# A 31-tap depthwise convolution: twenty taps on sixteen 32-wide tiles of TensorE instead of fourteen on four 64-wide ones

## The chip, the cores and the metric

The kernel runs on one core of one Trainium2 chip. The metric is the device time of one execution in microseconds, from a run's start to its end; lower is better. A profiled execution gives a trace with the start and duration of each instruction.

## What is computed

The program is a whole network of transformer-like layers in float32 on 512 tokens of 1024 channels. The change touches one stage of it, the convolution of a "conformer" block:

```python
y = pointwise(h)                       # 1024 -> 2 x 1024: value and gate
y = value * sigmoid(gate)              # "glu", channels x tokens
y = conv_general_dilated(y, w_dw, padding=15 + 15, feature_group_count=1024) + b_dw   # 31 taps, each channel alone
y = silu(layernorm(y)) ; y = pointwise2(y)
```

Each channel has 31 weights of its own. Output token t of a channel is the sum over j of weight j times input token t + j - 15.

## The kernel before

Channels lie on the 128 partitions and the 512 tokens along a row, so the 1024 channels are eight groups of 128, numbered g = 0 to 7. The parity p = g % 2 chooses one of two buffers. The stage is called `p_1` and each engine walks through the eight groups in its own order; semaphores tie the engines together.

**TensorE** computes the pointwise product in `linear` (L2315): for a group 48 matmuls of 128x128 by 128x512, because each float32 product is split in three (`w_hi*H_hi`, `w_hi*H_lo`, `w_lo*H_hi`). The results, value and gate, go to a pair of banks of the PSUM tensor `G`. Behind the linear of group g it runs `taps(g-1)` (L1986, L1989): fourteen of the 31 taps as matmuls whose stationary operand is a diagonal matrix of weights, `tap_diag`. The array is split in four tiles of 64x64. A tile that reads the lower 64 partitions and writes the upper ones needs its input turned by 64 partitions, which is what `yp_turned` holds. The order on TensorE is therefore linear(0), linear(1), taps(0), linear(2), taps(1), ..., linear(7), taps(6), taps(7). Two banks of the PSUM tensor `M` per parity hold the sums of the taps; `taps(g)` waits until VectorE has added up group g - 2 (semaphore `cv_d`).

**ScalarE** rounds the weights that DMA brought to `w_hi` (L507, two chunks a group, each when TensorE has used the slot two groups back), computes the sigmoid of the gate (L2037) and makes `yp_turned` by two copies of 64 partitions (L2042).

**VectorE** subtracts to get `w_lo` (L512, two a group), multiplies value and sigmoid into the padded input `yp` (L2122), computes the seventeen taps that TensorE doesn't (L2129, L2131 and fifteen at L2135, in two sums `Y` and `S[:, 2]`), and adds the sums up: the previous group's low bank of `M` (L2111), its own two sums (L2139), the previous group's second bank (L2117).

**GpSimd** builds the diagonals for a group with two instructions (L2281, L2284).

After group 7, VectorE adds taps(7), and TensorE sums all eight groups of `Y` over the channels for the layer norm (L1998). The layer norm's other steps follow, then the second pointwise product `p_2`. TensorE's queue is in program order, so L1998 stands behind taps(7).

Of the kernel before, what the change touches and what calls it, by code (L numbers as in the profile page):

```python
# [12 lines left out]
ALU = mybir.AluOpType  # L13
# [116 lines left out]
def build(nc, a, out, consts):  # L130

    plan, chunks = linear_plan()
    with ExitStack() as ctx:
# [31 lines left out]
        def small(name, shape, dt=F32):  # L165
            n = 4
            for s in shape[1:]:
# [75 lines left out]
              for e, places in enumerate(((188 * K, 190 * K, 192 * K, 194 * K), (196 * K, 198 * K, 200 * K, 173 * K)))]  # L243
# [4 lines left out]
        tap_diag = at("tap_diag", 117 * K, [P, 2, PE_TAPS, HP])  # L248
        yp_turned = at("yp_turned", 125 * K, [P, 2, T + 2 * PAD])
        taps_turned = at("taps_turned", 130 * K, [P, 8 * HALF_TAPS])  # L250
        half_ident = at("half_ident", 131 * K, [P, HP])
# [65 lines left out]
                             "fin_c").split()]  # L317

# [1629 lines left out]

        def second_pe(pe, linear, linear_units, norm, from_h, squares_behind):
# [24 lines left out]
            def taps(g, p):  # L1974

                if g == 1:
                    pe.wait_ge(mod_ok, 4)
                pe.wait_ge(cv_w, 2 * g + 2)
                wait_read(pe, "p_1", g)
                pe.wait_ge(cv_x, 2 * g + 4)  # L1980
                pe.wait_ge(cv_d, g + 1)
                low, high = slice(0, HP), slice(HP, P)
                for j in range(HALF_TAPS):
                    here, there = V_TAPS + j, V_TAPS + HALF_TAPS + j
                    for hs, bank in ((low, 2 * p), (high, 2 * p + 1)):
                        pe.matmul(M[hs, bank, :], tap_diag[hs, p, j, :], yp[hs, p, here:here + T], start=(j == 0),  # L1986
                                  stop=(j == HALF_TAPS - 1), skip_group_check=True)
                    for hs, other, bank in ((low, high, 2 * p), (high, low, 2 * p + 1)):
                        mm = pe.matmul(M[other, bank, :], tap_diag[hs, p, HALF_TAPS + j, :],  # L1989
                                       yp_turned[hs, p, there:there + T], start=(j == 0), stop=(j == HALF_TAPS - 1),  # L1990
                                       skip_group_check=True)
                mm.then_inc(cv_pe, 1)
# [19 lines left out]
        def second_act(act):  # L2012
# [22 lines left out]
            def glu(i, p, g):  # L2035
# [52 lines left out]
        def second_dve(dve, link):  # L2088
# [10 lines left out]
            dve.memset(yp_turned[:], 0.0)  # L2099
            link(dve.memset(yp[:], 0.0))  # L2100
# [6 lines left out]
            def total_low(g, p):  # L2107

                dve.wait_ge(cv_pe, g + 3)
                y = Y[:, g, :]  # L2110
                dve.tensor_tensor(y, y, M[:, 2 * p, :], ALU.add).then_inc(cv_a, 1)  # L2111

            def total_high(g, p):

                dve.wait_ge(cv_a, g + 1)
                y = Y[:, g, :]
                dve.tensor_tensor(y, y, M[:, 2 * p + 1, :], ALU.add).then_inc(cv_d, 1)  # L2117

            def glu(i, p, g):
# [25 lines left out]
            total_low(DT - 1, 1)  # L2145
# [563 lines left out]
```

## Time and profile before

| what | value |
|---|---|
| time, median of 3 runs (lowest to highest) | 2609.1 us (2605.2 to 2610.09) |
| the profiled execution: its own time, its span | 2605.56 us, 2603.6 us |
| TensorE busy in the span | 97% |
| VectorE, ScalarE, GpSimd busy | 59%, 39%, 4% |
| granted TensorE clock, mean | 0.99 |
| stage `p_1` with its taps and sums | 2028.4 to 2175.3 us of the span |

Busy times overlap, since a matmul's record contains its passage through the array: two records one behind the other can cover each other. What a matmul takes of TensorE is read from the distance between starts, not from its duration. The same holds for the other engines, where records of neighbours overlap by about 0.1 us.

### The profile page before, as it was taken

How to read it: one execution, taken by the hardware profiler on the slowest of the kernel's cores; microseconds unless marked ns; L12 is line 12 of the kernel's file. 1: busy time of each engine (PE TensorE's matmuls, PEld its weight loads, DVE VectorE, ACT ScalarE, POOL GpSimd, SP SyncE). 2: the span in 40 equal slices, each digit the busy share in tenths (PEclk: the TensorE clock that was granted, in tenths of full speed). 3: DMA queues.
4: the chain of work that ended last, by engine and by line, in shares of the span. 5: the costliest groups of instructions: out<-in, count | busy, mean ns of one | idle time of the engine just before them, and what ended most of it. 6: DMA issues, size and time to landing. Idle time of an engine off the chain costs nothing.

```text
span 2603.6 us, 31523 instructions
## 1 busy us (share of the span) xinstructions
PE 2526.5 (97%) x12548; PEld 2009.1 (77%) x12548; DVE 1539.9 (59%) x2574; ACT 1027.5 (39%) x1581; POOL 98.0 (4%) x133
## 2 busy tenths in 40 slices
PE   7999999999999989999998998999999999999999
PEld 6887788888886667888876875888888665888887
DVE  6455675877455656646665255666653997534433
ACT  4344543434435555433345345323223324422323
POOL 0000001010000000000000000011100110000000
PEclk9998999999999999999999998999999999999999
DMA  5422335554221122332324220366652221233331
GB/s 156 131 82 80 91 98 170 155 175 138 66 86 52 58 73 73 97 97 89 95 91 127 82 69 22 122 195 193 193 154 89 65 65 41 88 96 95 97 97 54
DMA packets 285081, 266.86 MB, mean 102 GB/s; under 512 B 13332, under 2 KB 270664, under 8 KB 284936
## 3 DMA queue, kind: packets, MB, share of 16 engines
q1 hardware_dynamic: 268503, 210.33, 26.3%
q0 software_dynamic: 15024, 54.33, 7.0%
q8 instruction: 99, 1.62, 0.3%
q14 instruction: 47, 0.38, 0.0%
q10 hardware_dynamic: 1408, 0.20, 0.0%
HBM read 262.72 MB, written 2.10 MB: 102 GB/s over the span
## 4 chain that ended last, share of the span: by engine, by line
PE 86%; DVE 8%; ACT 3%; issue 2%; SPq 1%; DMA 0%; POOL 0%; ACTq 0%; DVEq 0%; POOLq 0%
PE G L2315 70%; PE G L2331 7%; DVE Y L2135 2%; PE M L2384 1%; DVE S L2135 1%; DVE w_lo L512 1%; PE M L808 1%; PE M L818 1%; PE M L1171 1%; PE M L1182 1%; PE M L2365 1%; PE M L1655 1%; PE M L1193 1%; PE M L1644 0%; ACT w_hi L507 0%
## 5 line engine op out<-in xcount | busy, mean ns | idle before, releaser
L512 DVE TENSOR_TENSOR w_lo<-raw,w_hi 128x1024 fp32r<-128x1024 f32 x396 | 484.3, 1228 | 660.6 <-ACT w_hi L507 659.8
L2315 PE MATMUL G<-H_hi,w_hi 128*128 128x512 f32 (+1 forms) x2016 | 803.1, 398 | 5.6 <-DVE H_lo L375 1.6
L2315 PE MATMUL G<-H_hi,w_lo 128*128 128x512 f32 (+1 forms) x2016 | 783.8, 389 | 0.0
L2315 PE MATMUL G<-H_lo,w_hi 128*128 128x512 f32 (+1 forms) x2016 | 783.8, 389 | 0.0
L507 ACT ACTIVATE w_hi<-raw 128x1024 fp32r<-128x1024 f32 x396 | 417.3, 1057 | 911.2 <-PE G L2315 806.4
L2315 PEld LDWEIGHTS G<-H_hi,w_hi 128*128 128x128 f32 x2016 | 380.5, 189 | 110.0 <-issue 29.4
L2315 PEld LDWEIGHTS G<-H_hi,w_lo 128*128 128x128 f32 x2016 | 379.9, 188 | 79.3
L2315 PEld LDWEIGHTS G<-H_lo,w_hi 128*128 128x128 f32 x2016 | 380.5, 189 | 78.5 <-issue 4.6
L2315 PE MATMUL G<-hid_hi,w_hi 128*128 128x512 f32 x864 | 337.8, 391 | 5.3 <-DVE hid_lo L631 3.9
L2315 PE MATMUL G<-hid_hi,w_lo 128*128 128x512 f32 x864 | 336.9, 390 | 0.0
L2315 PE MATMUL G<-hid_lo,w_hi 128*128 128x512 f32 x864 | 336.8, 390 | 0.0
L2315 PEld LDWEIGHTS G<-hid_hi,w_hi 128*128 128x128 f32 x864 | 162.6, 188 | 42.0 <-DVE hid_lo L631 5.6
L2315 PEld LDWEIGHTS G<-hid_hi,w_lo 128*128 128x128 f32 x864 | 162.5, 188 | 33.9
L2315 PEld LDWEIGHTS G<-hid_lo,w_hi 128*128 128x128 f32 x864 | 162.7, 188 | 33.6
L2331 PE MATMUL G<-w_hi,H_hi 128*128 128x256 f32 x480 | 139.8, 291 | 1.4 <-DVE H_lo L463 1.3
L610 DVE SCALAR_TENSOR_TENSOR S<-SQ,VT,S 128x511 f32<-128x511 f32 (+1 forms) x176 | 128.2, 749 | 19.4 <-ACT S L572 16.3
L2331 PE MATMUL G<-w_lo,H_hi 128*128 128x256 f32 x480 | 136.3, 284 | 0.0
L2331 PE MATMUL G<-w_hi,H_lo 128*128 128x256 f32 x480 | 136.3, 284 | 0.0
L692 DVE SCALAR_TENSOR_TENSOR mod_acc<-mod_w,cs,mod_acc 128x512 f32<-128x512 f32 x168 | 125.9, 750 | 3.4
L670 POOL DMA_DIRECT2D mod_w<-in_w_mod x96 | 69.7, 726 | 1055.2 <-DVE mod_acc L692 470.6
L2331 PEld LDWEIGHTS G<-w_hi,H_hi 128*128 128x128 f32 x480 | 92.4, 193 | 12.5 <-DVE H_lo L463 5.9
L572 ACT ACTIVATE S<-SQ,VT 128x512 f32<-128x512 f32 x88 | 67.1, 810 | 88.2 <-DVE SQ L617 88.2
(347 smaller groups left out, 2427.7 us busy)
## 6 DMA issues: line engine op xcount, KB each, us to landing
raw<-in_w_ff SPq DMA_DIRECT2D x128, 512.0 KB
mod_w<-in_w_mod POOLq DMA_DIRECT2D x96, 512.0 KB, 4.5
raw<-in_ffn_w_up SPq DMA_DIRECT2D x176, 256.0 KB
raw<-in_ffn_w_down SPq DMA_DIRECT2D x32, 512.0 KB
raw<-in_w_in SPq DMA_DIRECT2D x28, 512.0 KB
raw<-in_mlstm_w_in SPq DMA_DIRECT2D x24, 512.0 KB
raw<-in_kv_w SPq DMA_DIRECT2D x16, 512.0 KB
raw<-in_fox_w_qg SPq DMA_DIRECT2D x16, 512.0 KB
```

The lines of the kernel that those rows point to most:

```text
L507: act.activation(w_hi[:, j, :], raw[:, j, :], ACT.Copy).then_inc(hi_done, 1)
L512: dve.tensor_tensor(w_lo[:, j, :], raw[:, j, :], w_hi[:, j, :], ALU.subtract).then_inc(lo_done, 1)
L572: act.activation(S[:, h, :], SQ[:, h, :], ACT.Identity, bias=VT[:, ds(t + cb, 1)], scale=VT[:, ds(t + (cw + 88), 1)]).then_inc(f_a, 1)
L610: return dve.scalar_tensor_tensor(S[:, h, k:T], SQ[:, h, 0:T - k], w, S[:, h, k:T], ALU.mult, ALU.add)
L670: pool.dma_start(mod_w[:, n % 2], src[:, 2 * quarter:2 * quarter + 2, block * 512:block * 512 + 512]).then_inc(mod_landed[n % 2], 16)
L692: one = dve.scalar_tensor_tensor(acc[:, cols], w, c, acc[:, cols], ALU.mult, ALU.add)
L808: return pe.matmul(M[:, bank, col:col + T - s * P], mK[hs, h // 2, s * P:s * P + P], mQ[hs, h // 2, s * P:T], start=(col == 0), stop=True, ...
L818: mm = pe.matmul(M[:, 2 + b // 2, (b % 2) * (P + 1):(b % 2 + 1) * (P + 1)], m_part(h, s)[:, (b - s) * P:(b - s) * P + P], mV[:, s, h, :], ...
L1171: mm = pe.matmul(fox_scores(n, e)[:, 0:(b + 1) * P], xQ[hs, q, b * P:b * P + P], xK[hs, q, 0:(b + 1) * P], start=True, stop=True)
L2135: link.post(dve.scalar_tensor_tensor(acc, yp[:, p:p + 1, j:j + T], tap(j), acc, ALU.mult, ALU.add))
L2315: mm = pe.matmul(G[:, 2 * p + m, 0:n], lw[:, k, ms], rh[:, t, 0:n], start=(t == 0 and q == 0), stop=(t == st["ktiles"] - 1 and q == 2), sk ...
L2331: mm = pe.matmul(G[:, 2 * p + b // 2, (b % 2) * GC:(b % 2) * GC + GC], lh[:, t, bs], rw[:, k, :], start=(t == 0 and q == 0 and b % 2 == 0) ...
```

## The change

TensorE takes twenty taps and VectorE eleven. The array is split in sixteen tiles of 32x32. For that there are four copies of the input, turned by 0, 32, 64 and 96 partitions; copy d carries five of the taps, and its tile reads quarter r of the partitions and writes quarter r + d, into bank r of `M`. All four banks of `M` serve one group, so `taps(g)` now waits for the sums of group g - 1. The copies turned by 32 and 96 are made by four DMAs that ScalarE issues, the one turned by 64 by two ScalarE copies as before. The diagonals, 128x32 each, are built by twenty ScalarE instructions a group, and GpSimd's part goes. VectorE adds four banks instead of two. Before the first group ScalarE makes a 32-wide identity and the turned weights in sixteen small instructions, where it had two.

```diff
-PE_TAPS = 14
-HALF_TAPS = PE_TAPS // 2
+COPIES, COPY_TAPS = 4, 5
+PE_TAPS = COPIES * COPY_TAPS
 V_TAPS = CONV_K - PE_TAPS
+QP = P // COPIES
...
-                pe.wait_ge(cv_w, 2 * g + 2)
+                pe.wait_ge(cv_w, g + 1)
                 wait_read(pe, "p_1", g)
-                pe.wait_ge(cv_x, 2 * g + 4)
-                pe.wait_ge(cv_d, g + 1)
...
-                for j in range(HALF_TAPS):
-                    here, there = V_TAPS + j, V_TAPS + HALF_TAPS + j
-                    for hs, bank in ((low, 2 * p), (high, 2 * p + 1)):
-                        pe.matmul(M[hs, bank, :], tap_diag[hs, p, j, :], yp[hs, p, here:here + T], start=(j == 0),
...
+                pe.wait_ge(cv_x, 2 * g + 2)
+                pe.wait_ge(cv_r[p], 64 * (g // 2 + 1))
+                pe.wait_ge(cv_d, g + 2)
+                for j in range(COPY_TAPS):
+                    for d in range(COPIES):
+                        source = yp_turned[d - 1] if d else yp
+                        tap = V_TAPS + COPY_TAPS * d + j
+                        for r in range(COPIES):
+                            rs, cs = quarter(r), quarter(r + d)
+                            mm = pe.matmul(M[cs, r, :], tap_diag[rs, p, COPY_TAPS * d + j, :], source[rs, p, tap:tap + T],
+                                           start=(j == 0), stop=(j == COPY_TAPS - 1), skip_group_check=True)
                 mm.then_inc(cv_pe, 1)
...
+                for d, parts in ((1, ((0, 96, 32), (96, P, 0))), (3, ((32, P, 0), (0, 32, 96)))):
+                    for first, end, source in parts:
+                        act.dma_start(yp_turned[d - 1][first:end, p, PAD:PAD + T],
+                                      yp[source:source + end - first, p, PAD:PAD + T]).then_inc(cv_r[p], 16)
                 for to, hs in ((slice(HP, P), slice(0, HP)), (slice(0, HP), slice(HP, P))):
-                    act.activation(yp_turned[to, p, PAD:PAD + T], yp[hs, p, PAD:PAD + T], ACT.Copy).then_inc(cv_x, 1)
...
+                    act.activation(yp_turned[1][to, p, PAD:PAD + T], yp[hs, p, PAD:PAD + T], ACT.Copy).then_inc(cv_x, 1)
+                for d in range(COPIES):
+                    for j in range(COPY_TAPS):
+                        col = ROW["w_dw_2"] + 8 * (V_TAPS + j) + g
+                        w = taps_turned[:, d - 1, 8 * j + g:8 * j + g + 1] if d else VT[:, col:col + 1]
+                        one = act.activation(tap_diag[:, p, COPY_TAPS * d + j, :], quarter_ident[:], ACT.Copy, scale=w)
+                one.then_inc(cv_w, 1)
+
+            for r in range(COPIES):
+                act.activation(quarter_ident[quarter(r), :], ident[quarter(r), quarter(r)], ACT.Copy).then_inc(cv_h, 1)
+                for d in range(1, COPIES):
+                    first = ROW["w_dw_2"] + 8 * (V_TAPS + COPY_TAPS * d)
+                    act.activation(taps_turned[quarter(r), d - 1, :], VT[quarter(r + d), first:first + 8 * COPY_TAPS],
+                                   ACT.Copy).then_inc(cv_h, 1)
+            act.wait_ge(cv_h, 16)
             groups(act, "p_1", split_hi, glu)
...
+            for tile in yp_turned + [yp]:
+                dve.memset(tile[:, :, 0:PAD], 0.0)
+                one = dve.memset(tile[:, :, PAD + T:], 0.0)
...
+            def total(g, r):
+
+                if r:
+                    dve.wait_ge(cv_a, 3 * g + r)
+                else:
+                    dve.wait_ge(cv_pe, g + 3)
                 y = Y[:, g, :]
...
                 if g:
-                    total_low(g - 1, 1 - p)
+                    total(g - 1, 0)
                 dve.tensor_tensor(y, y, other, ALU.add).then_inc(cv_v, 1)
                 if g:
-                    total_high(g - 1, 1 - p)
+                    for r in range(1, COPIES):
+                        total(g - 1, r)
...
             groups(dve, "p_1", split_lo, glu)
-            total_low(DT - 1, 1)
-            total_high(DT - 1, 1)
+            for r in range(COPIES):
+                total(DT - 1, r)
```

TensorE, where the linear of group 1 ends and taps(0) begins. A row's name is the source line, the instruction, what it writes and reads, the size of what it writes, and how many like it follow one another. Before:

```order
L2315 MATMUL G<-H_hi,w_hi 128x512
L2315 MATMUL G<-H_lo,w_hi 128x512
L2315 MATMUL G<-H_hi,w_lo 128x512
L1986 MATMUL M<-yp,tap_diag 64x512 x2
L1989 MATMUL M<-yp_turned,tap_diag 64x512 x2
```

and with the change, where the three turned copies bear the numbers 148 to 150:

```order
L2320 MATMUL G<-H_hi,w_hi 128x512
L2320 MATMUL G<-H_lo,w_hi 128x512
L2320 MATMUL G<-H_hi,w_lo 128x512
L1995 MATMUL M<-yp,tap_diag 32x512 x4
L1995 MATMUL M<-yp_turned_148,tap_diag 32x512 x4
L1995 MATMUL M<-yp_turned_149,tap_diag 32x512 x4
L1995 MATMUL M<-yp_turned_150,tap_diag 32x512 x4
```

The pair of tap rows stood seven times, 28 matmuls on four tiles; the four new tap rows stand five times, 80 matmuls on sixteen tiles. The linears are untouched.

ScalarE, from the last weight chunk before the stage on. Before:

```order
L507 ACTIVATE w_hi<-raw 128x1024
L2046 ACTIVATE taps_turned<-VT 64x56 x2
L507 ACTIVATE w_hi<-raw 128x1024 x2
L2037 ACT_TABLE_LOAD
L2037 ACTIVATE S<-G,VT 128x512
L2042 ACTIVATE yp_turned<-yp 64x512 x2
L507 ACTIVATE w_hi<-raw 128x1024 x2
```

and with the change, from the last of the four quarters of the small instructions on:

```order
L2060 ACTIVATE quarter_ident<-ident 32x32
L2063 ACTIVATE taps_turned<-VT 32x40 x3
L510 ACTIVATE w_hi<-raw 128x1024 x2
L2042 ACT_TABLE_LOAD
L2042 ACTIVATE S<-G,VT 128x512
L2048 DMA yp_turned_148<-yp 96x512
L2048 DMA yp_turned_148<-yp 32x512
L2048 DMA yp_turned_150<-yp 96x512
L2048 DMA yp_turned_150<-yp 32x512
L2051 ACTIVATE yp_turned_149<-yp 64x512 x2
L2056 ACTIVATE tap_diag<-quarter_ident,VT 128x32 x5
L2056 ACTIVATE tap_diag<-quarter_ident,taps_turned 128x32 x15
```

Sixteen small instructions now stand ahead of the stage's first weight chunk, and four DMA issues and twenty diagonals between a group's sigmoid and the next group's weight chunks.

VectorE, at the end of a group. Before:

```order
L2135 SCALAR_TENSOR_TENSOR S<-yp,VT,S 128x512
L2135 SCALAR_TENSOR_TENSOR Y<-yp,VT,Y 128x512
L2111 TENSOR_TENSOR Y<-Y,M 128x512
L2139 TENSOR_TENSOR Y<-Y,S 128x512
L2117 TENSOR_TENSOR Y<-Y,M 128x512
L512 TENSOR_TENSOR w_lo<-raw,w_hi 128x1024 x2
```

and with the change:

```order
L2156 SCALAR_TENSOR_TENSOR S<-yp,VT,S 128x512
L2156 SCALAR_TENSOR_TENSOR Y<-yp,VT,Y 128x512
L2134 TENSOR_TENSOR Y<-Y,M 128x512
L2160 TENSOR_TENSOR Y<-Y,S 128x512
L2134 TENSOR_TENSOR Y<-Y,M 128x512 x3
L515 TENSOR_TENSOR w_lo<-raw,w_hi 128x1024 x2
```

Two more additions of banks stand there, and of the rows of the first kind nine a group instead of fifteen.

## Rows read from the trace of the kernel before

**Rows 1.** The page, busy time of each engine: us, share of span, instructions.

```profile
PE 2526.5 (97%) x12548; PEld 2009.1 (77%) x12548; DVE 1539.9 (59%) x2574; ACT 1027.5 (39%) x1581; POOL 98.0 (4%) x133
```

**Rows 2.** taps(0) to taps(6): length, PE, PEld, DVE, ACT, POOL busy; PEclk, DMA, GB/s.

```profile
2050.37:2154.01 103.64, 103.64 (x625) 65.76 (x624) 103.18 (x142) 23.77 (x30) 13.86 (x12) 1.00 0.21 62
```

**Rows 3.** The timeline of TensorE around taps(4): start, duration, instruction, count.

```profile
2119.47 0.65 PE L1986 MATMUL M<-yp,tap_diag 64*64 64x512 f32 x2
...
2125.10 0.59 PE L1986 MATMUL M<-yp,tap_diag 64*64 64x512 f32 x2
2125.11 0.59 PE L1989 MATMUL M<-yp_turned,tap_diag 64*64 64x512 f32 x2
```

**Rows 4.** The timeline of VectorE over group 4.

```profile
2107.66 0.75 DVE L2122 SCALAR_TENSOR_TENSOR yp<-G,VT,S 128x512 f32<-128x512 f32 x1
2108.44 0.55 DVE L2129 TENSOR_SCALAR Y<-yp,VT 128x512 f32<-128x512 f32 x1
2108.90 1.18 DVE L2131 TENSOR_SCALAR S<-yp,VT 128x512 f32<-128x512 f32 x1
...
2119.32 0.73 DVE L2135 SCALAR_TENSOR_TENSOR S<-yp,VT,S 128x512 f32<-128x512 f32 x1
2119.99 0.73 DVE L2135 SCALAR_TENSOR_TENSOR Y<-yp,VT,Y 128x512 f32<-128x512 f32 x1
2120.75 0.69 DVE L2111 TENSOR_TENSOR Y<-Y,M 128x512 f32<-128x512 f32 x1
2121.36 0.68 DVE L2139 TENSOR_TENSOR Y<-Y,S 128x512 f32<-128x512 f32 x1
...
2122.56 2.36 DVE L512 TENSOR_TENSOR w_lo<-raw,w_hi 128x1024 fp32r<-128x1024 f32 x2
```

**Rows 5.** TensorE with four 32-wide column tiles, elsewhere in the program.

```profile
1970.71 2.78 PE L731 MATMUL M<-mod_acc,ones 128*32 128x512 f32 x24
```

**Rows 6.** TensorE with small matmuls in a row, elsewhere in the program.

```profile
1410.61 3.08 PE L1524 MATMUL G<-rm,sel 128*64 128x64 f32 x98
```

**Rows 7.** The timeline of ScalarE: small instructions at three places, then the stage's start.

```profile
104.15 0.40 ACT L954 ACTIVATE mL<-mN,gates_T 128x128 f32<-128x128 f32 x1
104.45 0.56 ACT L956 ACTIVATE mL<-M,gates_T 128x384 f32<-128x384 f32 x1
...
689.52 1.57 ACT L2539 ACTIVATE xV<-G,root_T 128x256 f32<-128x256 f32 x4 [5.98 <-DVE root_T L2619]
...
2037.29 0.53 ACT L2046 ACTIVATE taps_turned<-VT 64x56 f32<-64x56 f32 x2
...
2039.66 1.06 ACT L507 ACTIVATE w_hi<-raw 128x1024 fp32r<-128x1024 f32 x1 [0.75 <-PE G L2315]
...
2042.04 0.69 ACT L2037 ACTIVATE S<-G,VT 128x512 f32<-128x512 f32 x1
2043.99 1.29 ACT L2042 ACTIVATE yp_turned<-yp 64x512 f32<-64x512 f32 x2 [1.27 <-DVE yp L2122]
```

**Rows 8.** DMAs that ScalarE issues: timeline of two issues; size and landing.

```profile
1.61 0.34 ACTq L2186 DMA_DIRECT2D v_rows<-in_norm_mix_pre  x1
1.98 0.44 ACTq L2186 DMA_DIRECT2D v_rows<-in_norm_mix_post  x1
...
ident<-const_ident ACTq DMA_DIRECT2D x1, 64.0 KB, 3.9
```

**Rows 9.** The timeline of TensorE at the stage's end.

```profile
2161.49 0.65 PE L1986 MATMUL M<-yp,tap_diag 64*64 64x512 f32 x2 [1.23 <-ACT yp_turned L2042]
...
2167.66 6.28 PE L1998 MATMUL G<-Y,ones 128*128 128x512 f32 x14
2174.12 1.13 PE L1998 MATMUL G<-Y,ones 128*128 128x512 f32 x2 [0.19 <-DVE Y L2117]
```

**Rows 10.** Stretches around an idle TensorE, columns as in rows 2.

```profile
1370.70:1374.20 3.50, 0.01 (x1) 0.00 (x0) 2.36 (x2) 1.02 (x4) 2.95 (x6) 1.00 0.56 132
1375.30:1378.60 3.30, 3.30 (x11) 2.27 (x10) 0.08 (x1) 1.32 (x2) 0.00 (x0) 0.50 0.86 344
```

More of the change, by code:

```diff
@@ L247, in build @@
         yp = at("yp", 112 * K, [P, 2, T + 2 * PAD])
[L248 to L251, printed above, removed]
+        yp_turned = [at(f"yp_turned{d}", 117 * K + 4608 * (d - 1), [P, 2, T + 2 * PAD]) for d in range(1, COPIES)]
+        tap_diag = at("tap_diag", 131 * K, [P, 2, PE_TAPS, QP])
+        taps_turned = at("taps_turned", 136 * K + 128, [P, COPIES - 1, 8 * COPY_TAPS])
+        quarter_ident = at("quarter_ident", 137 * K, [P, QP])
         G = ctx.enter_context(nc.psum_tensor("G", [P, 4, 512], F32))
@@ L317, in build @@
                              "fin_c").split()]
+        cv_r = [sem(f"cv_r{p}") for p in range(2)]
         TOKENS = [(hid_l, 1), (cv_pe, 2), (cv_d, 2)]
@@ L2098, in second_dve @@
             dve.wait_ge(chunk_used, used_after("s0_down3"))
-            dve.memset(yp_turned[:], 0.0)
-            link(dve.memset(yp[:], 0.0))
+            for tile in yp_turned + [yp]:
+                dve.memset(tile[:, :, 0:PAD], 0.0)
+                one = dve.memset(tile[:, :, PAD + T:], 0.0)
+            link(one)
             dve.wait_ge(mod_ok, 3)
@@ L2105, in second_dve @@
             mod_rest(dve, link, 1)
-            def total_low(g, p):
-                dve.wait_ge(cv_pe, g + 3)
-                y = Y[:, g, :]
[L2111 to L2117, printed above, removed]
+            def total(g, r):
[3 more added lines that the diff above has]
+                    dve.wait_ge(cv_pe, g + 3)
+                y = Y[:, g, :]
+                one = dve.tensor_tensor(y, y, M[:, r, :], ALU.add)
+                if r == COPIES - 1:
+                    one.then_inc(cv_d, 1)
+                else:
+                    one.then_inc(cv_a, 1)
             def glu(i, p, g):
@@ L2269, in _ @@
             pool_mod(pool)
-            pool.wait_ge(chunk_used, used_after("s0_down3"))
-            taps = VT[:, ROW["w_dw_2"]:ROW["w_dw_2"] + 8 * CONV_K].rearrange("p (j t) -> p j t", t=8)
-            turned = taps_turned[:].rearrange("p (j t) -> p j t", t=8)
-            pool.tensor_tensor(half_ident[:], ident[:, 0:HP], ident[:, HP:P], ALU.add).then_inc(cv_h, 1)
-            pool.wait_ge(cv_h, 1)
-            pool.wait_ge(cv_x, 2)
-            each = half_ident[:].unsqueeze(1).to_broadcast([P, HALF_TAPS, HP])
-            for t in range(DT):
-                p = t % 2
-                pool.wait_ge(cv_pe, t + 1)
-                pool.tensor_tensor(tap_diag[:, p, 0:HALF_TAPS], each,
-                                   taps[:, V_TAPS:V_TAPS + HALF_TAPS, t:t + 1].to_broadcast([P, HALF_TAPS, HP]),
-                                   ALU.mult).then_inc(cv_w, 1)
-                pool.tensor_tensor(tap_diag[:, p, HALF_TAPS:PE_TAPS], each,
-                                   turned[:, :, t:t + 1].to_broadcast([P, HALF_TAPS, HP]),
-                                   ALU.mult).then_inc(cv_w, 1)
         @block.tensor
```

12 lines of the change are left out of this document (2 added, 10 removed).

## The prediction

> **What bounds the kernel now.** I read the busy times first [rows 1]: TensorE is busy 97% of the span and no other engine over 59%, so over the whole program TensorE's own work sets the time. The stage has a balance of its own. Between the starts of taps(0) and taps(6), six groups, TensorE is busy 103.64 of 103.64 us and VectorE 103.18, at full clock [rows 2]. Both are full, so neither may lose work alone and save much. A group takes 103.64 / 6 = 17.27 us.
>
> In the timeline of TensorE [rows 3] taps(4) starts at 2119.47 and its last burst at 2125.10. Fourteen bursts, four records on the four tiles within some 0.02 us, are thirteen distances of (2125.10 - 2119.47) / 13 = 0.433, so I take 0.43 a burst. A float32 matmul goes through in two passes, hence seven tap rounds are fourteen bursts: 14 x 0.43 = 6.02. The rest of the group, linear and the two changes of tiling, is 17.27 - 6.02 = 11.25 us.
>
> In VectorE's timeline [rows 4] a tap costs 0.66 from start to start (2119.32 to 2119.99) and an addition 0.61. L2131 takes 1.18 where a like one needs some 0.45, since GpSimd builds diagonals at that moment. The whole group is, in distances of starts: 0.78 for yp, 0.46, 0.39, 0.7 of that disturbance, 15 x 0.663 = 9.95, 0.1 until the last tap is written, 3 x 0.6 = 1.8 and 2.3 for the two w_lo: 16.5. So VectorE is 0.8 us shorter than TensorE, and TensorE decides the group.
>
> **TensorE's part of the change.** 80 matmuls in two passes on sixteen tiles are ten bursts instead of fourteen, if all sixteen tiles run at once. The nearest row is L731 [rows 5]: four column tiles of 32, each with an input of its own, 24 records in 2.78 us. With 0.6 for the last one, five distances of (2.78 - 0.6) / 5 = 0.436: four different inputs stream at the same time from the same partitions at no loss. Rows of different quarters at once are what the 64-wide tiles do already [rows 3]. Both ways together are in no row; I take 0.43 a burst, 4.30, and 0.08 more for starting sixteen tiles one behind the other. Upper bound by issue: L1524 [rows 6] issues 98 records in 3.08 us, (3.08 - 0.22) / 97 = 29.5 ns a record together with its weight load; 160 of them would be 4.72. The page of the Trainium skill "TensorE: Matmul & The Clock Gate", Part 3, measured sixteen 32x32 tiles at 10.6 times the speed of one, one burst and not float32; it speaks for full overlap, and by it the sum stays as it is.
>
> The group becomes 11.25 + 4.38 = 15.63, which saves 1.64. Over six distances: 9.8 us.
>
> **Does another engine stand in the way of 15.63?** VectorE loses six taps (6 x 0.663 = 3.98) and GpSimd's 0.7 and gains two additions. The last two wait for the write of the one before, so 0.72 each instead of 0.6: 16.5 - 3.98 - 0.7 + 1.44 = 13.3. ScalarE has, a group: sigmoid 0.67, two w_hi 2.1, copies 1.3 [rows 7], four DMA issues at 0.37, the distance in [rows 8], 1.5, and twenty diagonals. A 128x32 instruction with a weight per partition is in no row. L954, 128x128 with such an operand, stands 0.30 before its neighbour, and L2539 does 256 columns in (1.57 - 0.46) / 3 = 0.37 [rows 7]. The difference is 0.0006 a column, so 32 columns are 0.24 us, or less where the fixed part is smaller; I take 0.2, 4.0 for twenty; bounds 0.1 and 0.3. Together 9.6 of 15.6. The new wait for group g - 1 is a ring too: taps(g), linear(g+2), w_hi 1.1, w_lo 1.2, VectorE's group 11.0, and only then taps(g+2): 4.4 + 11.2 + 2.3 + 11.0 = 28.9 for two groups, 14.5 each. Nothing there reaches 15.63. The DMAs land 3.9 us after issue [rows 8], while taps(g) comes over 10 us after yp(g): hidden.
>
> **The start.** The sixteen small instructions stand ahead of the first w_hi. Two of 64x56 took 0.53 [rows 7], so I take 0.24 each, 3.8 instead of 0.5. Behind them ScalarE had 0.75 of idle time before the second w_hi, and sigmoid ended at 2042.73 for a yp that started at 2043.22. So yp(0) comes 3.3 - 0.75 - 0.5 = 2.05 late, at 2045.3, and ends at 2046.05. Then DMA issues 1.5, copies 1.3, diagonals 4.0: 2052.8, when linear(1) has ended at 2050.3. taps(0) starts 2.4 late. The landing of the DMAs (2047.6 + 3.9 = 2051.5) is just below. Memsets are shorter by some 1.5 us, but VectorE waits there for the norm's row.
>
> taps(6) then starts at 2052.8 + 6 x 15.63 = 2146.6 instead of 2154.01: 7.4 earlier.
>
> **The end**, where I expect the gain to be given back. Before, taps(7) ran at 2161.49 under VectorE's last group, and fourteen of the sixteen records of L1998 under it as well; from taps(6) to the last sum went 2175.25 - 2154.01 = 21.2 us [rows 9]. With the change taps(7) must wait until VectorE has emptied `M` of group 6, which it does at the end of its group 7. From the start of taps(6), when linear(7) has just ended: w_hi and w_lo 2.4, VectorE's group 0.78 + 0.46 + 0.39 + 5.97 + 0.1 + 0.6 + 0.6 + 0.6 + 1.44 = 10.9, so 13.3 until taps(7), then 4.4 bare, and then L1998 with all sixteen records, 15 x 0.43 + 0.6 = 7.05, since it is queued behind taps(7). VectorE's four last additions, 2.7, lie beside L1998. Sum 24.75.
>
> TensorE is idle for 13.3 - 4.4 = 8.9 us before taps(7). After 3.5 us without work at 1370.7 the granted clock of the next stretch is 0.50, the lower of the two levels, and it stays there for 3.4 us [rows 10]. So taps(7) begins at half clock, for 3.4 to 6.8 us, of which half is lost: 1.7 to 3.4, I take 2.5. The same page of the skill, Part 1, says that an idle TensorE falls to 1.2 GHz and comes back when busy; the trace agrees. The end takes 27.2, 6.0 more than before.
>
> **Sum.** -7.4 + 6.0 = -1.4 us. Against the profiled execution's own 2605.56 that is 2604.2. The median of the runs, 2609.1, lies 3.5 above that execution, and the runs span 4.9, so I put the forecast at 2609.1 - 1.4, about 2607.5. A measurement of this kernel can tell 0.2%, 5.2 us, from nothing.
>
> Bounds of the likeliest case. Issue at 29.5 ns instead of 26.9: 0.42 x 7 = +2.9. Diagonals at 0.3: +2; at 0.1: -1.3, since the DMAs land then. Small instructions at 0.1: -2 (not both, PE is ready at 2050.3; together -2.4). DMA issues at 0.5 (the longer record of [rows 8] is 0.44): +0.5. Clock: -0.8 or +0.9. From -1.4 this gives -4.6 to +4.9, all within 0.2%. Chance 0.54.
>
> **Rivals.** (a) Sixteen tiles do not overlap fully. L731 shows four column tiles, L1986 two by two; should only eight run at once, there are twenty bursts, 8.6 us, and with 4.3 more in seven places the kernel takes +30, 2638. From a burst of 0.48 on (seven times 0.5 = 3.5 more, with the upper ends above) it is slower. Full halving 0.10; a partial loss, 0.5 to 0.55 a burst, +5 to +8, 0.13. (b) The instructions aren't brought up in time. The skill's same page, Part 1, gives some 62 ns a matmul where microcode decodes. As a mechanism here: 160 records at 62 ns are 9.9 us, 5.5 more in seven places, +39, 2647; the 29.5 ns of [rows 6] speak against it, 0.03. (c) Faster: the start is hidden (taps(0) at 2050.4, -2.4) and the low clock falls to its short end or away (-0.8 to -2.5): -4.6 to -6.3, and a little less per burst passes the mark; 2602. For it speaks that full-width small instructions overlap by 0.1 us; against it that two partial ones did not. 0.19. (d) ScalarE becomes late with w_hi: with issues of 0.5 and diagonals of 0.3 its group is 0.67 + 2.1 + 1.3 + 2.0 + 6.0 = 12.1, still under 15.6. w_hi would be 1 to 2 us late in a group that has over 2 to spare: 0.01 beyond the mark. (e) A cost nobody sees in these rows, such as more waits on TensorE or DMA traffic against `raw`: in the range.
>
> So faster 0.19, same 0.54, slower 0.27. The likeliest case spans 2603 to 2614.5; with the partial loss of (a) and with (c) the range that leaves out two in ten is 2601 to 2617.
>
> **What would show it.** In the profile after: starts of taps(1) to taps(6) 15.6 us apart; sixteen records within about 0.1 us and bursts 0.43 apart; a taps(7) that waits for VectorE's L2134 and lies bare before L1998 at clock 0.50; diagonals 0.2 apart; the first taps near 2052.8. I am wrong if a burst takes over 0.48, if TensorE waits for VectorE or ScalarE within the six groups, or if the clock stays at full level in the end.

## The result and the profile after

The changed kernel takes 2614.55 us (median of 8 runs, 2612.26 to 2616.71), the kernel before 2605.48 (8 runs, 2604.84 to 2610.09). The ratio is 1.003, with a 95% interval of 1.0019 to 1.0041: slower by 0.3%, some 9 us. The forecast was 2607.5 and no measurable change. It was counted from 2609.1, the median of three runs; from the 2605.48 of eight the same sum, -1.4, gives 2604.1, so the miss is some 10 us. The execution that was profiled is the longest of the eight, span 2614.9 against 2603.6; where its other microseconds lie is said below.

The page of the changed kernel first, its busy times (us, share of the span, instructions), to be held against [rows 1]:

```profile
PE 2525.2 (97%) x13380; PEld 2016.7 (77%) x13380; DVE 1509.8 (58%) x2548; ACT 1064.0 (41%) x1755; POOL 77.7 (3%) x116
```

TensorE has 832 records more and 1.3 us less of busy time, VectorE 30 us less. Nothing of that can be read as time, so I went to the stage. TensorE's timeline of the changed kernel, the group of taps(4) from its first burst to the next linear (start, duration, instruction, count, and in brackets the idle time before it and what ended it):

```profile
2125.05 0.63 PE L1995 MATMUL M<-yp,tap_diag 32*32 32x512 f32 x4
2125.08 0.69 PE L1995 MATMUL M<-yp_turned,tap_diag 32*32 32x512 f32 x12
2125.50 0.61 PE L1995 MATMUL M<-yp,tap_diag 32*32 32x512 f32 x4
2125.53 0.66 PE L1995 MATMUL M<-yp_turned,tap_diag 32*32 32x512 f32 x12
2125.93 0.83 PE L1995 MATMUL M<-yp,tap_diag 32*32 32x512 f32 x4
2126.18 0.79 PE L1995 MATMUL M<-yp_turned,tap_diag 32*32 32x512 f32 x12
...
2127.01 0.82 PE L1995 MATMUL M<-yp,tap_diag 32*32 32x512 f32 x4
2127.23 0.80 PE L1995 MATMUL M<-yp_turned,tap_diag 32*32 32x512 f32 x12
...
2130.50 0.50 PE L2320 MATMUL G<-H_hi,w_hi 128*128 128x512 f32 x1
```

The first two bursts are as the prediction has them: sixteen records (4 + 12) within 0.1 us, the next sixteen 0.45 later. So sixteen tiles do stream at once. From the third burst on they don't begin together any more: of the four records of `yp` the first begins at 2125.93, on time, the other three from 2126.13 on (the row lasts 0.83 instead of 0.61), and the twelve of `yp_turned` from 2126.18. From there a round of sixteen tiles, two bursts, takes 1.05 to 1.06 (2126.18 to 2127.23) and not 0.86, so 0.20 more. The taps take 2130.50 - 2125.05 = 5.45 us, where the prediction has 4.38. Before it was 6.17 up to the next linear (2119.47 in [rows 3] to 2125.64): fourteen bursts of 0.43, 6.02, and some 0.15 for the change to the linear. Counted like that the new taps are ten bursts, 4.30, the same 0.15, and 1.0 that is new.

The weight loads show what is late. A load that stands alone, on time, and the next one:

```profile
2125.94 0.10 PEld L1995 LDWEIGHTS M<-yp,tap_diag 32*32 32x32 f32 x1 [0.33 <-issue]
2126.12 0.10 PEld L1995 LDWEIGHTS M<-yp,tap_diag 32*32 32x32 f32 x1
```

Each late matmul begins 4 ns after the start of its load. Their turn, 0.43 behind the burst before, was at 2125.93 to 2126.03, so they wait for their weights.

The same kernel's start and end in TensorE's timeline: the first linear, the first records of taps(0) and taps(7), and the sums; taps(1) begins at 2075.39 and taps(6) at 2158.16.

```profile
2031.26 0.47 PE L2320 MATMUL G<-H_hi,w_hi 128*128 128x512 f32 x1 [0.64 <-DVE H_lo L378]
...
2057.28 1.08 PE L1995 MATMUL M<-yp,tap_diag 32*32 32x512 f32 x4 [4.00 <-ACT tap_diag L2056]
...
2171.75 1.08 PE L1995 MATMUL M<-yp,tap_diag 32*32 32x512 f32 x4 [8.08 <-DVE Y L2134]
...
2179.43 7.13 PE L2003 MATMUL G<-Y,ones 128*128 128x512 f32 x16
```

Two waits are new, 4.00 us ahead of taps(0) for ScalarE's diagonals and 8.08 ahead of taps(7) for VectorE's totals. The records behind either last 1.08 instead of 0.63: the clock is low. The windows view says it too (length, then busy time of TensorE, its weight loads, VectorE, ScalarE, GpSimd, granted clock, DMA share, GB/s):

```profile
2057.30:2060.60 3.30, 3.30 (x64) 1.20 (x65) 2.32 (x3) 2.40 (x3) 0.00 (x0) 0.50 0.02 6
2075.39:2158.16 82.77, 82.77 (x1042) 58.82 (x1041) 65.96 (x95) 41.08 (x125) 0.00 (x0) 1.00 0.32 94
...
2171.75:2176.60 4.85, 4.85 (x89) 2.15 (x97) 0.00 (x0) 0.00 (x0) 0.00 (x0) 0.50 0.01 3
```

The second row is five groups at full clock: TensorE busy throughout, VectorE 65.96 of 82.77. Before, both were full [rows 2]. VectorE is off the bound, and 82.77 / 5 = 16.55 is TensorE's own group.

**Where the time went**, in stretches of the profiled executions, with linear(0) at 2028.42 before and 2031.26 after:

| stretch | before | after | difference |
|---|---|---|---|
| linear(0) to taps(0) | 21.95 | 26.02 | +4.07 |
| taps(0) to taps(1) | 17.27 | 18.11 | +0.84 |
| taps(1) to taps(6), five groups | 86.37 | 82.77 | -3.60 |
| taps(6) to the end of the sums | 21.24 | 28.41 | +7.17 |
| together | 146.83 | 155.31 | +8.5 |

The 8.5 agree with the 9 us between the medians. The span has 2.8 more ahead of linear(0), and that isn't the change's: in the profiles of the variants below linear(0) starts anywhere from 2027.01 to 2031.54, with the same TensorE program ahead of it. The granted clock of earlier stages differs from one execution to the next. Of 165 us from 1305 on, its mean is 0.99 in the profile before and 0.97 in the one after. The same hole in the same program shows how: an idle time of 2.21 us near 1404, first before, then after.

```profile
1403.16 3.40 PE L2384 MATMUL M<-SQ,ones 128*128 128x512 f32 x7 [2.21 <-ACT SQ L442]
```

```profile
1405.55 1.22 PE L2389 MATMUL M<-SQ,ones 128*128 128x512 f32 x1 [2.21 <-ACT SQ L445]
```

Behind it the granted clock is 1.00 before and 0.50 after (windows 1405.3 to 1408.7). Of the fourteen profiles of this case six have it full there and eight low, though what they differ in comes 600 us later. So I compare stretches counted from linear(0) between profiles, and totals only over many runs.

### The profile page after: what moved, and what is told of

The parts are those of the page before. It is cut to its first block, busy times and chain, and to the rows that moved or that the text cites. A ratio compares the mean times of both kernels' runs of the same rounds, so it can differ in the third digit from the quotient of the medians.

```text
span 2614.9 us, 33348 instructions
## 1 busy us (share of the span) xinstructions
PE 2525.2 (97%) x13380; PEld 2016.7 (77%) x13380; DVE 1509.8 (58%) x2548; ACT 1064.0 (41%) x1755; POOL 77.7 (3%) x116
## 4 chain that ended last, share of the span: by engine, by line
PE 90%; DVE 4%; ACT 3%; issue 2%; SPq 1%; DMA 0%; ACTq 0%; POOL 0%; DVEq 0%; POOLq 0%
PE G L2320 73%; PE G L2336 7%; PE M L1995 2%; PE M L2389 1%; PE M L811 1%; PE M L821 1%; PE M L1185 1%; PE M L1174 1%; PE M L1196 1%; PE M L2370 1%; PE M L1658 1%; ACT w_hi L510 1%; PE M L1647 0%; DVE S L613 0%; PE M L2395 0%
```

## Experiments on the taps

Three questions stood after the result: why a group's taps take 5.45 and not 4.38, what the start costs, what the end costs. "Issue" means here that TensorE can't take in its instructions faster; "overlap" that sixteen tiles stream more slowly than four.

**Half the columns.** This kernel leaves out TensorE's twenty taps for the second half of the tokens.

```diff
-  mm = pe.matmul(M[cs, r, :], ..., source[rs, p, tap:tap + T],
+  mm = pe.matmul(M[cs, r, 0:GC], ..., source[rs, p, tap:tap + GC],
```

> The tap matmuls stream 256 columns instead of 512, so half of every token row gets no TensorE taps (part of the computation is left out); everything else is as with the change. It asks what sets the 5.45 us that 80 tap matmuls take where 4.3 were forecast. Theory (issue): behind the first two bursts TensorE gets a record with its weight load only every 33.4 ns, whatever it streams, so 160 records still take 4.4 to 5.4 us from the first tap to the next linear. Rival (overlap): sixteen tiles streaming at once slow each other, on the input side or in PSUM; half the columns are then half the time, about 2.7 us.

The first record and the next linear, in its TensorE timeline:

```profile
2068.89 0.42 PE L1995 MATMUL M<-yp,tap_diag 32*32 32x256 f32 x4
...
2072.20 0.50 PE L2320 MATMUL G<-H_hi,w_hi 128*128 128x512 f32 x1
```

3.31 us, neither of the two. Both theories fell as I had stated them. The two points fit a cost per column and a fixed part: (5.45 - 3.31) / 256 columns = 8.36 ns for the 160 records together, 4.28 at 512, which is ten bursts of 0.43; and 1.17 beside it. Of that 0.15 is the change to the linear that the kernel before has too; the other 1.0 is 0.20 for each of the five rounds. (The group of taps(5) took 3.95 there at full clock, which I can't explain; the other full-clock ones are alike.)

**A quarter of the columns**, `0:P` in the same place, tests that line with a third point; it leaves out three quarters of the tokens.

> As the half-column run, with 128 of 512 columns streamed (three quarters of every row get no TensorE taps, part of the computation left out). 512 columns took 5.45 us from the first tap to the next linear and 256 took 3.32, so neither pure issue nor pure overlap loss holds. Theory (additive): the tiles stream as forecast, 8.3 ns a column over ten bursts, and 1.19 us are fixed, 0.24 for each of the five rounds of sixteen tiles, because the next round's weight loads come up late: 2.26 us. Rival (supply): a record with its weight load needs at least some 20.7 ns, which 256 columns just reached: 3.3 us again.

```profile
2070.93 0.31 PE L1995 MATMUL M<-yp,tap_diag 32*32 32x128 f32 x4
...
2073.19 0.50 PE L2320 MATMUL G<-H_hi,w_hi 128*128 128x512 f32 x1
```

2.26. The line gives 1.17 + 128 x 0.00836 = 2.24. And 160 records with their loads go in 2.26 us, 14 ns each, half of the 29.5 that I had worked out of [rows 6] as a bound of issue: that row never was one for small tiles. The late rows of `yp_turned` agree without the line: from the second round on they follow each other 0.63 apart with 256 columns and 0.42 with 128, where two bursts of the stream are 0.43 and 0.21. The surplus is 0.20 a round at all three widths. (Two of the six full-clock groups took 4.1; in one of them TensorE has a hole of 1.54 us ahead of the last thirteen records, put down to issue. I left it there.)

It doesn't follow the clock either. In the kernel with early totals, below, taps(0) ran at half clock (0.50 from 2054.9 to 2060.7), and two rounds follow each other like this:

```profile
2056.84 1.24 PE L1995 MATMUL M<-yp_turned,tap_diag 32*32 32x512 f32 x12
...
2058.77 1.24 PE L1995 MATMUL M<-yp_turned,tap_diag 32*32 32x512 f32 x12
```

That is 1.93, where two bursts take 1.70 at this clock: a surplus of 0.23, not of 0.40.

**Eight tiles at a time.** The computation is complete; the loop goes twice over the five taps, for d = 0, 1 and for d = 2, 3.

```diff
-  for j in range(COPY_TAPS):
-      for d in range(COPIES):
+  for half in range(2):
+      for j in range(COPY_TAPS):
+          for d in (2 * half, 2 * half + 1):
```

> The same 80 tap matmuls in another order: two halves, each five rounds over eight tiles, so that only eight tiles can run at once; the computation is complete. It asks what the fixed 0.24 us a round hang on. Theory (a round of sixteen tiles holds 64 instructions, weight loads and matmuls of two passes, and TensorE sees only a limited number of them ahead, so the next round's loads begin late): with eight tiles the next round is always within reach, twenty bursts of 0.43 and almost nothing on top, 8.6 to 8.8 us from the first tap to the next linear. Rival (every burst pays for starting its tiles one behind the other, 0.12 for sixteen): half of that for eight, twenty times 0.49, 9.8 us. Either way the kernel becomes slower, by 7 times 3.2 us or more.

```profile
2094.49 0.63 PE L1996 MATMUL M<-yp,tap_diag 32*32 32x512 f32 x4
...
2096.66 0.61 PE L1996 MATMUL M<-yp,tap_diag 32*32 32x512 f32 x4
...
2102.64 0.50 PE L2322 MATMUL G<-H_hi,w_hi 128*128 128x512 f32 x1
```

Five bursts in 2096.66 - 2094.49 = 2.17, 0.434 each, and all records of a burst begin on time. 8.15 for the twenty bursts is less than 20 x 0.434, since the second half's tiles begin under the end of the first. With eight tiles the first half shows no surplus at all.

**Twelve tiles.** This one leaves out the five taps of the last copy.

```diff
-  for d in range(COPIES):
+  for d in range(COPIES - 1):
```

> Leaves out the five taps of the third turned copy (d = 3): a round has twelve tiles, five rounds, 120 records a group. Question: to what does the 0.24 us belong that a round of sixteen tiles takes beyond its two bursts (1.09 against 0.86), and that a round of eight does not take. Theory A, the reach of the queue: the loads of the next round come late because a round of sixteen puts 64 instructions (32 loads, 32 matmuls) between a tile's matmul and its next load; a round of twelve has 48, and the surplus is gone or small: 5 x 0.87 = 4.35 us from the first record to the next linear, at most 4.6. Rival B, a cost per tile above eight: half the surplus, 0.12 a round, about 4.95 us. Rival C, a cost of every round in which all four row quarters and all four column quarters carry three or more tiles: the whole surplus, 5.45 us. The time itself says little, since taps(7) and the end keep their chain.

```profile
2091.12 0.63 PE L1995 MATMUL M<-yp,tap_diag 32*32 32x512 f32 x4
2091.15 0.66 PE L1995 MATMUL M<-yp_turned,tap_diag 32*32 32x512 f32 x8
...
2092.01 0.60 PE L1995 MATMUL M<-yp,tap_diag 32*32 32x512 f32 x4
2092.03 0.88 PE L1995 MATMUL M<-yp_turned,tap_diag 32*32 32x512 f32 x8
...
2092.86 0.61 PE L1995 MATMUL M<-yp,tap_diag 32*32 32x512 f32 x4
...
2095.98 0.50 PE L2320 MATMUL G<-H_hi,w_hi 128*128 128x512 f32 x1
```

4.86, by the number rival B's (4.95), by the rows neither's. The rounds begin 0.85 to 0.89 apart (2091.12, 2092.01, 2092.86), so no round loses anything; but from the second round on part of the tiles begin late (the row of eight records lasts 0.88 instead of 0.66), and that lag is paid once, at the end: 4.86 - 5 x 0.86 - 0.15 = 0.41. With sixteen the lag is paid in every round. So twelve tiles keep the 0.43 of a burst and sixteen don't. Per record sixteen are still faster, 34.1 ns over a group to 40.5, where 0.43 a burst would be 27. The reach of the queue had forecast at most 4.6 here: it fits the rhythm of the rounds and misses the lag at the end.

**Another order of the sixteen**: along rows of the array instead of diagonals, the rest as it was, computation complete.

```diff
-  for d in range(COPIES):
-      ...
-      for r in range(COPIES):
+  for r in range(COPIES):
+      for d in range(COPIES):
```

> Complete computation; within a round of sixteen tiles the order alone is changed: four tiles of one row quarter follow one another (columns r, r+1, r+2, r+3), where the changed kernel walks along diagonals. The number of instructions between a tile's matmul and its next load stays 64. Theory A (reach of the queue): nothing changes, 5.45 us a group from the first record to the next linear (5.35 to 5.55). Rival C (the surplus comes from tiles that follow one another on different rows and columns, or from output banks written by turns): the surplus goes or doubles, 4.4 or over 5.8 us. Time as the changed kernel by A, 2614 within 4.

5.45 from the first record to the next linear (2075.34 to 2080.79), as by the reach of the queue; rival C's other order does nothing. One run, 2616.81 us.

**Where the loads stop.** In the second round the loads pause behind the first tiles, and they begin again 0.03 us after the first record of the second burst has ended, counted from a group's first record: at 1.07 for 1.04 with 512 columns, at 0.65 for 0.62 with 256, at 0.43 for 0.40 with 128, at 1.94 for 1.91 at half clock, and with twelve tiles again at 1.07 for 1.04, each time with 33 or 34 loads begun. With eight tiles the first half has no such pause. So in these rows the loads wait for a matmul of the round before to be finished, which is what a limited reach of the queue would do. No run changes that reach alone, so it stays the likeliest reading and not a shown one.

## Experiments on the start and the end

**The totals of group g - 1 between VectorE's own taps**, so that `M` comes free earlier:

```diff
   link.post(dve.scalar_tensor_tensor(acc, yp[...], tap(j), acc, ...))
+  if g and 4 <= j < 8:
+      total(g - 1, j - 4)
 ...
-  if g:
-      total(g - 1, 0)
 ...
-  if g:
-      for r in range(1, COPIES):
-          total(g - 1, r)
```

> VectorE adds the four banks of the previous group between its own taps 4 to 8, each behind one tap, instead of at the end of the group; the same work. Theory (the end is a serial chain: VectorE's last group, bare taps(7), sums): taps(7) starts about 10.5 us after taps(6) instead of 13.6, the end shrinks by about 3 us, and the six groups before don't change, since TensorE sets them (16.55 each). Against the changed kernel -3 to -4 us, that is a ratio to the kernel before of about 1.002. Rival (the end is set by TensorE's sixteen sums and the low clock): taps(7) comes earlier but the low clock covers the same stretch, less than 1 us.

2613.71 us (7 runs, 2612.43 to 2615.34), ratio to before 1.0027 [1.0017, 1.0037]: hardly a gain over the changed kernel's 1.003, where 3 to 4 us were expected. From taps(6) to the sums' end 26.66 instead of 28.41, so 1.75 less, and taps(7) begins 12.0 behind taps(6) and not 10.5. Its timeline of ScalarE, last group, and the first row of taps(7) in TensorE's:

```profile
2160.06 3.06 ACTq L2048 DMA_DIRECT2D yp_turned<-yp  x4
...
2164.48 1.17 ACT L2056 ACTIVATE tap_diag<-quarter_ident,VT 128x32 f32<-128x32 f32 x5
2165.55 3.27 ACT L2056 ACTIVATE tap_diag<-quarter_ident,taps_turned 128x32 f32<-128x32 f32 x15
```

```profile
2168.88 1.08 PE L1995 MATMUL M<-yp,tap_diag 32*32 32x512 f32 x4 [6.48 <-ACT tap_diag L2056]
```

VectorE is done with `M` at 2167.37, but now taps(7) waits for ScalarE until 2168.82. Behind the wait that I cured stood another, which ends 1.45 us later: 3.06 us of DMA issues, 1.3 of copies and 4.3 of diagonals.

**The sums of blocks 0 to 5 ahead of taps(7)**, in the idle time:

```diff
+  if g == DT - 1:
+      wait_read(pe, "p_1", DT - 2)
+      group_sums(0, DT - 2)
 ...
-  for t in range(DT): ...
+  group_sums(DT - 2, DT).then_inc(cv_s, 1)
```

> TensorE computes the layer norm's sums over groups 0 to 5 in the idle time ahead of taps(7), and only those of groups 6 and 7 behind it; the same work. Theory (queue order and clock): 12 of 16 records of 0.43 us leave the bare end, and TensorE rests under 3.5 us, so that the granted clock stays at its upper level: from taps(6) to the last sum 28.4 us become about 22.9, VectorE's four additions being last. Against the changed kernel -5 to -6 us, ratio to before about 1.001. Rival: VectorE's additions set the end already and the clock stays low: -1 us.

2611.10 us (12 runs, 2607.13 to 2614.46), 1.0016 [1.0007, 1.0025]. The end takes 25.62. Its TensorE timeline:

```profile
2162.53 5.42 PE L1983 MATMUL G<-Y,ones 128*128 128x512 f32 x12
2170.67 1.08 PE L2004 MATMUL M<-yp,tap_diag 32*32 32x512 f32 x4 [2.72 <-DVE Y L2139]
...
2177.54 1.13 PE L1983 MATMUL G<-Y,ones 128*128 128x512 f32 x2
2180.63 2.08 PE L1983 MATMUL G<-Y,ones 128*128 128x512 f32 x2 [1.96 <-DVE Y L2139]
```

Six of eight sums are off the end, 5.4 us, but 2.8 net remain of it, and 5 to 6 were expected. The expectation that under 3.5 us of rest the clock would stay up was wrong: taps(7) begins at half clock after 2.72 us of idle time, and takes 6.87 for 5.45. The last sum now waits 1.96 for the last total, and it runs at half clock too, 2.08 for two records where the two ahead of it took 1.13.

**ScalarE's sixteen small instructions between the fills of `H_hi`**, two behind each, instead of ahead of the first group's w_hi:

```diff
+  for t in range(DT):
+      fill_act(act, "odd", ..., (t,))
+      ...  # two of quarter_ident and taps_turned
-  for r in range(COPIES):
-      act.activation(quarter_ident...)
-      ...
```

> The sixteen small ScalarE instructions stand two by two in the gaps of the fill before the stage instead of in one row ahead of the first weight chunk; the same work. [...] Against the changed kernel -3 to -5 us. Rival: the fill has no room (gaps of 0.6 us for two instructions of 0.25), the linear starts later by what the taps win: 0.

**The four DMAs of a group from GpSimd's queue** instead of ScalarE's:

```diff
 (act)  -  act.dma_start(yp_turned[d - 1]..., yp...)
 (pool) +  for g in range(DT):
        +      wait_read(pool, "p_1", g); pool.wait_ge(cv_pe, g + 1)
        +      ...  pool.dma_start(yp_turned[d - 1]..., yp...)
```

> GpSimd, idle here, issues the four DMAs of a group instead of ScalarE; the same work. They took 2.5 to 3.3 us of ScalarE's time where the forecast had 1.5. Theory: at the start the chain yp(0), issues, copies, diagonals loses its 2.5 us, so taps(0) starts 2 to 2.5 us earlier (a little less if GpSimd's own issue and landing then decide), the six groups stay at 16.62 us from taps to taps, the end stays too, since VectorE decides it: -2 to -3 us against the changed kernel, ratio to before about 1.002. Rival: landing is late from GpSimd's queue and takes the place of the issues: 0.

2610.27 us (11 runs, 2607.00 to 2613.15), 1.0016 [1.0008, 1.0025], and 2609.52 (11 runs, 2606.88 to 2611.28), 1.0013 [1.0004, 1.0022]. The first row of taps(0) in the timeline of the one and of the other:

```profile
2051.99 0.63 PE L1995 MATMUL M<-yp,tap_diag 32*32 32x512 f32 x4 [1.46 <-ACT tap_diag L2067]
```

```profile
2052.03 0.63 PE L1995 MATMUL M<-yp,tap_diag 32*32 32x512 f32 x4 [1.43 <-ACT tap_diag L2052]
```

Each alone brings taps(0) from 26.02 to 23.50 and 23.46 behind linear(0). The second gain is the clock: after an idle time of 1.4 us it stays at full level (0.63 for the row of four records), after 4.00 it had fallen, and taps(0) to taps(1) is 16.56 and 16.58 instead of 18.11. The two gains together are 4.1 us in either kernel.

**Sixteen taps on TensorE**, four of each copy, `COPY_TAPS = 4`, fifteen on VectorE; complete.

> Four taps a copy instead of five: TensorE takes sixteen taps, VectorE fifteen; nothing else. Theory (round of sixteen tiles 1.09 us, stream 0.86 plus 0.23): taps take 4 x 1.09 = 4.4 us on TensorE, whose group would be 15.5; VectorE's is 13.3 + 4 x 0.66 = 15.9 and decides: 15.9 to 16.1 from taps to taps instead of 16.55. ScalarE builds sixteen diagonals: the start is 0.9 earlier. The end: VectorE's last group 2.6 longer, taps(7) 1.1 shorter. Against the changed kernel -3.3 - 0.9 + 1.5 = -2 to -4 us. Rival (the ring through the new wait for group g - 1 decides: taps, linear, w_hi, w_lo, VectorE's group of 13.6): over 16.5 a group and 0 or slower in all.

2611.95 us (11 runs, 2608.05 to 2614.71), 1.0019 [1.0010, 1.0028]. The taps take 4.38, and 5.45 - 4.38 = 1.07 is one round less, as the surplus says. But taps(1) already waits for VectorE, and taps(2) too:

```profile
2072.48 0.63 PE L1995 MATMUL M<-yp,tap_diag 32*32 32x512 f32 x4 [1.92 <-DVE Y L2134]
...
2088.37 0.63 PE L1995 MATMUL M<-yp,tap_diag 32*32 32x512 f32 x4 [0.31 <-DVE Y L2134]
```

The group is 79.47 / 5 = 15.89, VectorE's and not 15.5, and the end grows to 30.08, since VectorE's last group has four taps more. taps(0) has 3.07 us of idle time ahead of it; its first 0.8 us run at full clock and the next 3.4 at half, so the clock fell behind the hole and not in it.

**All four cures at once**, with twenty taps and with sixteen; the edits are those above.

> Twenty taps on sixteen tiles as changed, with the four cures together: totals early, sums of groups 0 to 5 first, small instructions in the fill's gaps, DMAs from GpSimd. Theory (start and end gave the gain back, the six groups keep 0.7 us each): start as before the change, six groups -4.3, end 20 to 21.5 instead of 21.2: -4 to -5 us against the kernel before, ratio 0.998 to 0.9985. Rival (the cures overlap in what they cure, and the low clock takes the rest): within 0.1% of before.

> The four cures and sixteen taps instead of twenty on TensorE. Theory: start as before the change, six groups of 15.95 instead of 17.27, -7.9 us, end about 19.6 to 21 instead of 21.2: -8 to -9.5 us against the kernel before, ratio 0.9965 to 0.997. Rival (VectorE, now full, is slowed by its neighbours or by the ring): groups of 16.5, ratio 0.9985.

Twenty taps: 2602.26 us (11 runs, 2599.99 to 2604.05), ratio to before 0.9987 [0.9978, 0.9996]. Sixteen: 2602.07 (11 runs, 2598.57 to 2606.68), 0.9986 [0.9977, 0.9995]. Both are faster than the kernel before by 3 us, a small gain that the interval just sets apart from none, and by the ratios some 11 us faster than the changed kernel. With twenty taps 4 to 5 us below the kernel before were expected; the stretches of the profile give 4.8, the medians 3.3. With sixteen, 8 to 9.5 were expected, and that missed. The end with twenty, then with sixteen:

```profile
2148.44 0.63 PE L2004 MATMUL M<-yp,tap_diag 32*32 32x512 f32 x4
...
2153.89 5.42 PE L1983 MATMUL G<-Y,ones 128*128 128x512 f32 x12
2159.24 0.63 PE L2004 MATMUL M<-yp,tap_diag 32*32 32x512 f32 x4
...
2164.69 1.12 PE L1983 MATMUL G<-Y,ones 128*128 128x512 f32 x2
2167.77 1.37 PE L1983 MATMUL G<-Y,ones 128*128 128x512 f32 x2 [1.96 <-DVE Y L2140]
```

```profile
2161.23 1.08 PE L2004 MATMUL M<-yp,tap_diag 32*32 32x512 f32 x4 [5.66 <-DVE Y L2140]
```

With twenty, taps(6), the early sums and taps(7) join without a hole and at full clock; the end takes 20.70. With sixteen the group is shorter (77.70 / 5 = 15.54), but VectorE, whose own group is 15.76, is late at the end: taps(7) waits 5.66 and begins at half clock, 26.11. So the two come out alike.

The stretches of all complete kernels, us; the total runs from linear(0) to the end of the sums:

| kernel | to taps(0) | to taps(1) | to taps(6) | to the sums' end | total |
|---|---|---|---|---|---|
| before | 21.95 | 17.27 | 86.37 | 21.24 | 146.83 |
| changed | 26.02 | 18.11 | 82.77 | 28.41 | 155.31 |
| totals early | 26.05 | 19.26 | 82.77 | 26.66 | 154.74 |
| sums first | 26.04 | 19.30 | 82.77 | 25.62 | 153.73 |
| small ones earlier | 23.50 | 16.56 | 82.77 | 28.77 | 151.60 |
| DMAs from GpSimd | 23.46 | 16.58 | 82.77 | 28.47 | 151.27 |
| eight tiles | 26.03 | 20.88 | 96.31 | 31.63 | 174.85 |
| sixteen taps | 25.11 | 19.00 | 79.47 | 30.08 | 153.66 |
| four cures, 20 | 21.97 | 16.55 | 82.77 | 20.70 | 141.99 |
| four cures, 16 | 21.98 | 15.50 | 77.70 | 26.11 | 141.29 |

In the two rows with 19.26 and 19.30 the clock was low at taps(0) for 6.8 us and not for the 3.4 of the changed kernel's profile, behind the same wait of 4.0; the edits there don't touch it. It makes their totals 1.2 us too long.

## Why the prediction was wrong

The sum said -1.4; counted the same way it is +8.5. It forecast no measurable change, and the kernel became slower by 9 us. The 9.9 between the sums, step by step:

- **"I take 0.43 a burst, 4.30, and 0.08 more": the step that failed.** Sixteen tiles stream at once, as said, but each round costs 0.20 beside its two bursts, and the 0.08 was meant for the whole group: 5.45 for 4.38, of which 0.15 is the change to the linear that my 11.25 already held. A group is 16.55 where 15.63 was forecast, 0.92 in each of six distances, +5.5, and once more in the end, +1.07. My upper bound, 4.72 from the rate of [rows 6], didn't cover it, because that rate has nothing to do with this case: the quarter-column kernel goes at 14 ns a record. It is rival (a) in its partial form, 0.545 a burst, to which I gave 13 in 100 and +5 to +8.
- **The rule on sixteen tiles.** The rows above show one burst of sixteen complete, its records starting over 0.10 us, and the third one broken. The Trainium skill, "TensorE: Matmul & The Clock Gate", Part 3, measured one burst, and for one burst the trace agrees with full overlap. Rounds one behind the other are not in it, and I carried it over to them. What its 10.6 of sixteen means for a row of rounds I didn't ask.
- **The start, 2.4 late: the right chain, too short.** It is 4.07. The four DMA issues took 2.53 where I had four distances of 0.37, +1.0; the diagonals 4.35 for 4.0, the small instructions 4.1 for 3.8. Together +1.65. ScalarE's timeline of the changed kernel:

```profile
2040.25 0.75 ACT L2063 ACTIVATE taps_turned<-VT 32x40 f32<-32x40 f32 x3
...
2048.99 2.53 ACTq L2048 DMA_DIRECT2D yp_turned<-yp  x4
...
2052.88 1.17 ACT L2056 ACTIVATE tap_diag<-quarter_ident,VT 128x32 f32<-128x32 f32 x5
2053.96 3.27 ACT L2056 ACTIVATE tap_diag<-quarter_ident,taps_turned 128x32 f32<-128x32 f32 x15
```

- **A term that I had not seen.** I asked what an idle TensorE does to the clock at the end and not at the start, though there too I had it idle for 2.5 us. taps(0) ran at half clock, +1.55. That this comes from the wait is shown: the eight profiles with a wait of 4.0 all have low clock at taps(0), and both kernels that cut it to 1.4 us have taps(0) at full clock.
- **The end: right in its waits, its clock and its sums.** The wait for `M` was 13.3 and is 13.60; the clock's loss 2.5 and is 7.68 - 5.45 = 2.23; the sums 7.05 and are 7.13. The taps in it carry the failed term: 28.41 for 27.2. The 3.4 to 6.8 us that I had given the low clock was an estimate; it lasted 4.85 us of taps(7).
- **No other engine in the way of a group: right.** VectorE is busy 65.96 of 82.77, 13.2 a group as forecast (13.3), and every wait of TensorE lies at the start and the end.

Together 5.5 + 1.65 + 1.55 + 1.15 = 9.9. So the mechanism of loss that I described, a gain in the middle given back at both ends, is what happened; the middle was worth 4.3 with taps(0)'s group (6 x 0.72) and not 9.8.

Shown: the surplus per round with sixteen tiles at three widths, two counts of rounds and both levels of the clock, that rounds of eight and twelve don't lengthen, the order's indifference; that the loads are what is late; the two waits and the clock behind each; that curing both ends turns 1.003 into 0.9987. Only argued: why the loads are late. That 64 instructions lie between a tile's matmul and its next load, more than TensorE looks ahead, agrees with where the loads stop, but it had forecast less for twelve tiles (4.35 to 4.6, measured 4.86), and none of the kernels changes that reach alone. Left open: the few groups with narrow columns that took 0.6 to 1.9 us more, and what decides the level of the clock behind a short hole, at 1405 us as in the stage.

## What to carry to other kernels

More tiles at once pay as long as the rounds keep their rate: read the start-to-start time of the third and fourth round, never of the first burst, where here twelve small tiles kept it and sixteen took a quarter more (over a whole group sixteen still led, 34 ns a record to 40.5). A cheaper step in the middle of a pipeline is worth what its first and last pass leave of it, so write out the chain of the first and of the last group, with each engine's queue, before the sum of the middle; work that can be done early (sums of blocks that are ready, constants) belongs in their holes. The holes of 2.7 us or more in this stage cost themselves and 1.4 to 2.7 us more for the clock; since such holes stand behind one another, four cures that shorten the stage by 1.7, 2.8, 3.7 and 4.0 us, 12.2 in all with the longer low clock at taps(0) in two of them left out, were worth 13.3 together.

## What was not expected of the hardware

- A round of sixteen 32x32 tiles in float32 takes 1.06 us from the second round on, of twelve 0.86, of eight 0.87. Records of one burst begin 6.7 ns apart, late ones 17 ns.
- Four issues of DMAs from 32 and 96 partitions to others took ScalarE 2.53 us in the first group and 3.06 in the last (of the kernel with early totals), 0.63 to 0.77 each, about twice the 0.37 of [rows 8].
- In the stage the clock was low after idle times of 2.72, 4.00, 5.66, 6.48 and 8.08 us and full after 1.43 and 1.46. Between them the same hole went either way: after 2.21 us near 1405 it was low in eight profiles and full in six, and after the 1.96 us ahead of the last sum it was low in the kernel with the sums first and full in both kernels with all four cures, in one of them for 0.7 us only. Behind 3.07 us it was full for 0.8 us and then low.
